# Attention in a hybrid decoder step: keys of the last branch unmasked, scores on quarter tiles, its projections in three pieces spread over later steps

## The chip, the core and the metric

One core of one Trainium2 chip runs the whole program. The metric is the device time of the program in microseconds, as the median of several runs. The trace is of one profiled execution. Engines: TensorE (PE, with its weight loads PEld), VectorE (DVE), ScalarE (ACT), GpSimd (POOL), and SyncE (SP), which issues most DMAs. Each engine runs its own list of instructions in order; semaphores tie the lists together.

## What is computed

Two layers over a prompt of 1024 tokens and 8 sample tokens, model width 1024, float32. Layer one is a gated delta rule with an MLP, and is not touched. Layer two is the attention treated here, and then an MLP of width 4096. The attention has three branches (window, dilation) = (128, 1), (512, 4), (2048, 16). Each has 8 query heads of width 64 in 2 groups that share one key and value head each:

```
q = (h @ w_q).reshape(N, L, N_BRANCH, KV_HEADS_B, GQA_B, HEAD_DIM_B)
s = einsum('nqhgd,nqkhd->nqhgk', q_blk, kg) * scale + bias      # keys at distance 0, d, .., window
p = exp(s - lse);  o = einsum('nqhgk,nqkhd->nqhgd', p, vg)
out = sum over branches of softmax(lse) * o;  mix = out @ w_o
```

`bias` is the slope of the head times the distance. With the dilation taken out by reordering the tokens by their residue, a query tile of 128 tokens reads one or two key tiles of 128 tokens.

## The kernel before

**Dense products.** A product of 128 output features is made for one of three pieces of the 1032 token columns (`CUTS`: 352, 352, 328). It has 8 k-steps (`KT`) of three matmuls each: high part of the weight by high and by low part of x, low part of the weight by high part of x. Weights stream from memory as units of 4 k-tiles x 512 columns in two halves into `w_raw`; `split_hi` (ScalarE, L603) and `split_lo` (VectorE, L1113) multiply by the gain and split them into a ring of 4 slots, `w_hi` and `w_lo`. `take` (VectorE, L1802) moves a finished product out of PSUM: keys to `k_mask`, values to `v_feat`, queries to `q_stage`, from where SP stores them to memory (`store_query`), and `load_query` brings a tile of 128 queries back as `q_tile`.

**Steps.** The attention runs in 26 steps. Step i treats query tile i in the order of `tile_of` (L99): 0 to 7 are branch 2 (one key tile each), 8 to 15 branch 1 (one key tile at even, two at odd), 16 to 23 branch 0 (16 has one key tile, the others two). The two halves `hs` of a tile are 4 heads each. For a tile: `scores` (TensorE, L2599) multiplies queries and keys, into PSUM banks 3 and 4; `biased` (VectorE, L1868) adds the bias and writes `prob`; `maxima` takes the row maxima; `exps` (ScalarE) the exponentials; `turn` (TensorE, L2614) transposes the probabilities into banks 5 and 6; `turned` copies them to `prob_t` (bank 5 ScalarE, bank 6 VectorE); `apply` (TensorE, L2622) multiplies with V into bank 7; `keep_outputs` (ScalarE, L989) copies to `out_t`, and `outputs_turn` transposes it back. From step 19 on `merge_turn` adds the merging of the three branches. TensorE's order within a step, written out by hand from L2679 on, is: turn half 0 of the tile before, scores half 1 of this tile, outputs_turn, fill, turn half 1, scores half 0 of the next tile, fill, apply, fill.

**Keys.** `k_mask` holds the keys twice, once per group, with zeros in the other group's 64 rows. One matmul of 128 rows by 128 queries then gives the scores of both groups side by side: 256 columns for one key tile and 512 for two. A call makes two of these (j). With one key tile both share a bank (3 for half 0, 4 for half 1); with two, each has its own, which VectorE frees singly.

**Fills.** There are three places per step, numbered 3 x step, + 1, + 2. `dense_done(place)` says how many k-steps of the remaining 30 products are done by then: 96 in places 0 to 17 (queries of branch 1), then 6 per place until 240 are done at place 41, in step 13. `GROUPS` orders them: queries of branch 1, queries of branch 0, keys and values of branch 0. They rotate over PSUM banks 0 to 2. From place 66 on (step 22) the fills are the output projection (`output_done`, L2575), whose weights, units 10 and 11 counted from `U_KVQ`, `SPLITS` splits at the end of steps 12 to 15. `LOADS` names the weight halves that SP loads at each step.

**The 8 samples.** Their single query is treated beside the steps: `samples_queries` (VectorE, step 14) signals `dense_done`, on which SP loads their keys, values and bias (1.8 MB) over x_hi; then come `samples_keys` and `samples_scores` (16), `samples_maxima` (16), `samples_shares` (17), `samples_turn` (18), `samples_apply` and `samples_outputs` (19). `decode_done` lets SP bring back x (`x_b`, 4.1 MB) in step 20. `store_keys(0)` follows in SP's list of step 14.

## Time and profile before

| | us |
|---|---|
| median of 3 runs (2721.39 to 2723.74) | 2722.85 |
| the profiled execution | 2721.97 |
| its span | 2720.2 |

Granted clock of TensorE over the span: 0.991 of 2.4 GHz. The attention's steps begin in the trace at these times (the first `turn` of a step, or for step 0 its first `scores`):

| step | 0 | 6 | 8 | 14 | 15 | 16 | 17 | 18 | 19 | 20 | 21 | 22 |
|---|---|---|---|---|---|---|---|---|---|---|---|---|
| us | 1632.17 | 1695.54 | 1721.41 | 1808.88 | 1818.63 | 1830.17 | 1849.10 | 1856.74 | 1870.20 | 1881.81 | 1894.05 | 1903.67 |

How to read the rows further down. A row of windows has the stretch, its length, then the busy time of PE, PEld, DVE, ACT and POOL with the number of instructions, the granted clock of PE as a share of 2.4 GHz, the busy share of the DMA engines and GB/s. In a timeline one fp32 matmul has two records, so `x4` is two matmuls; records of a pipelined engine overlap, so the time of a group is best read from the start of one to the start of the next. In the chain each row is start, duration and what ran or was waited for. SPq is the queue of DMA issues of SP.

### The profile page before, as it was taken

The page shows a single profiled execution, that of the slowest core. Times are in us where ns is not written, and L with a number is a line of the kernel's source. Part 1 is how long each engine was busy: PE and PEld are TensorE (multiplying, and loading weights), DVE is VectorE, ACT ScalarE, POOL GpSimd, SP SyncE. Part 2 cuts the span into 40 slices and gives each one's busy share as a digit, 9 for nine tenths or more (in the row PEclk, how much of TensorE's full clock was granted, in tenths as well). Part 3 has the DMA queues.
Part 4 walks back from the last instruction along what each step waited for, and adds up shares of the span by engine and source line. Part 5 has one row for each costly group of instructions (what it writes and reads, how often), then busy time and mean ns, then how long its engine had stood idle before and what let it go on. Part 6 is the DMA issues. An engine that isn't in the chain of part 4 may idle for free.

```text
span 2720.2 us, 48302 instructions
## 1 busy us (share of the span) xinstructions
PE 2638.9 (97%) x20476; PEld 2508.2 (92%) x20476; DVE 1553.1 (57%) x2961; ACT 827.6 (30%) x1870; POOL 66.6 (2%) x92
## 2 busy tenths in 40 slices
PE   7999999997899999999999999988999999999998
PEld 6999999996699999999999998864899999999997
DVE  6777777777575444444444736567764444444445
ACT  5444544543141211121112314345531112111211
POOL 0000000000300000000000000002200000000000
PEclk9999999998999999999999999998999999999999
DMA  3111101134311111111111234334111111111111
GB/s 142 48 42 41 41 20 32 34 119 164 106 47 63 47 47 39 56 47 47 40 55 47 97 101 118 96 116 134 59 47 47 47 47 47 47 47 47 47 32 63
DMA packets 81989, 174.32 MB, mean 64 GB/s; under 512 B 21681, under 2 KB 46801, under 8 KB 81060
## 3 DMA queue, kind: packets, MB, share of 16 engines
q1 hardware_dynamic: 73860, 162.72, 18.5%
q10 hardware_dynamic: 7920, 8.56, 1.0%
q8 instruction: 162, 2.65, 0.4%
q14 instruction: 47, 0.39, 0.0%
HBM read 140.28 MB, written 36.21 MB: 65 GB/s over the span
## 4 chain that ended last, share of the span: by engine, by line
PE 89%; DVE 5%; DMA 2%; ACT 1%; issue 1%; POOL 1%; SPq 0%; DVEq 0%; ACTq 0%; POOLq 0%
PE psum L2085 19%; PE psum L2086 19%; PE psum L2087 19%; PE psum L2159 4%; PE psum L2160 4%; PE psum L2161 4%; PE psum L2111 2%; PE psum L2358 2%; PE psum L2609 2%; PE psum L2567 1%; PE psum L2632 1%; PE psum L2568 1%; PE psum L2569 1%; PE psum L2450 1%; DMA x_half<-in_x 1%
## 5 line engine op out<-in xcount | busy, mean ns | idle before, releaser
L2085 PE MATMUL psum<-x_hi,w_hi 128*128 128x352 f32 (+1 forms) x1040 | 334.8, 322 | 0.0
L2086 PE MATMUL psum<-x_lo,w_hi 128*128 128x352 f32 (+1 forms) x1040 | 332.4, 320 | 0.0
L2087 PE MATMUL psum<-x_hi,w_lo 128*128 128x352 f32 (+1 forms) x1040 | 330.9, 318 | 0.0
L1118 DVE SCALAR_TENSOR_TENSOR w_lo<-w_raw,gains,w_hi 128x512 fp32r<-128x512 f32 x380 | 262.1, 746 | 84.7 <-ACT w_hi L608 84.6
L608 ACT ACTIVATE w_hi<-w_raw,gains 128x512 fp32r<-128x512 f32 x380 | 246.9, 712 | 121.5 <-DMA w_raw<-in_w 121.2
L2159 PE MATMUL psum<-x_hi,w_hi 128*128 128x352 f32 (+1 forms) x768 | 273.2, 356 | 1.2 <-DVE pre L1200 1.2
L2085 PE MATMUL psum<-u_hi_b,w_hi 128*128 128x352 f32 (+1 forms) x768 | 247.1, 322 | 0.0
L2085 PE MATMUL psum<-u_hi,w_hi 128*128 128x352 f32 (+1 forms) x768 | 246.7, 321 | 0.0
L2085 PE MATMUL psum<-x_hi_b,w_hi 128*128 128x352 f32 (+1 forms) x768 | 246.6, 321 | 0.0
L2160 PE MATMUL psum<-x_lo,w_hi 128*128 128x352 f32 (+1 forms) x768 | 245.9, 320 | 0.0
L2086 PE MATMUL psum<-x_lo_b,w_hi 128*128 128x352 f32 (+1 forms) x768 | 245.5, 320 | 0.0
L2161 PE MATMUL psum<-x_hi,w_lo 128*128 128x352 f32 (+1 forms) x768 | 245.2, 319 | 0.0
L2087 PE MATMUL psum<-u_hi_b,w_lo 128*128 128x352 f32 (+1 forms) x768 | 245.2, 319 | 0.0
L2087 PE MATMUL psum<-u_hi,w_lo 128*128 128x352 f32 (+1 forms) x768 | 245.2, 319 | 0.0
L2086 PE MATMUL psum<-u_lo_b,w_hi 128*128 128x352 f32 (+1 forms) x768 | 245.0, 319 | 0.0
L2086 PE MATMUL psum<-u_lo,w_hi 128*128 128x352 f32 (+1 forms) x768 | 245.0, 319 | 0.0
L2087 PE MATMUL psum<-x_hi_b,w_lo 128*128 128x352 f32 (+1 forms) x768 | 244.3, 318 | 0.0
L1742 DVE SCALAR_TENSOR_TENSOR relu<-psum,rs 128x352 f32<-128x352 f32 (+1 forms) x192 | 99.1, 516 | 214.2 <-PE psum L2087 206.7
L908 ACT ACTIVATE u_hi_b<-relu 128x352 fp32r<-128x352 f32 (+1 forms) x96 | 47.2, 492 | 519.4 <-DVE relu L1745 519.4
L908 ACT ACTIVATE u_hi<-relu 128x352 fp32r<-128x352 f32 (+1 forms) x96 | 47.2, 492 | 516.8 <-DVE relu L1745 516.8
L2086 PEld LDWEIGHTS psum<-x_lo,w_hi 128*128 128x128 f32 x1040 | 195.5, 188 | 0.5
L2085 PEld LDWEIGHTS psum<-x_hi,w_hi 128*128 128x128 f32 x1040 | 195.4, 188 | 0.5
(373 smaller groups left out, 5542.4 us busy)
## 6 DMA issues: line engine op xcount, KB each, us to landing
w_raw<-in_w SPq DMA_DIRECT2D x190, 512.0 KB, 3.7
q_tile<-scratch_q SPq DMA_DIRECT2D x24, 256.0 KB, 3.0
scratch_att<-o_out ACTq DMA_DIRECT2D x32, 132.0 KB, 2.5
x<-in_x SPq DMA_DIRECT2D x8, 516.0 KB, 9.8
s_state<-in_s_rec_in SPq DMA_DIRECT2D x2, 2048.0 KB, 14.7
out_s_rec<-s_state SPq DMA_DIRECT2D x8, 512.0 KB, 2.6
merge<-scratch_att SPq DMA_DIRECT2D x8, 512.0 KB, 3.7
scratch_o_heads<-head_out ACTq DMA_DIRECT2D x7, 512.0 KB, 2.7
```

The costliest lines, as they stand in the source:

```text
L608: done = act.activation(w_hi[:, slot, 2 * part + k], w_raw[:, part, k], ACT.Copy, scale=gains[:, unit * UW + 2 * part + k:unit * UW + 2 * ...
L908: act.activation(lay.u_hi[:, tile, THIRDS[third]], relu[:, 0:width(third)], ACT.Copy).then_inc(sem("u_hi_ready"), L.add("u_hi_ready"))
L1118: done = v.scalar_tensor_tensor(w_lo[:, slot, 2 * part + k], w_raw[:, part, k], gains[:, unit * UW + 2 * part + k:unit * UW + 2 * part + k ...
L1742: v.scalar_tensor_tensor(r, psum[:, TAKES[n % 6], 0:width(third)], 0.0, rs[:, cols], ALU.max, ALU.mult).then_inc(sem("product_free"), L.ad ...
L2085: mm(out, whi, xh[:, k, cols], start=k == 0, stop=False)
L2086: mm(out, whi, xl[:, k, cols], start=False, stop=False)
L2087: done = mm(out, wlo, xh[:, k, cols], start=False, stop=k == kts - 1)
L2111: done = nc.tensor.transpose(psum[0:cols, bank, at_col:at_col + rows], src, ident[0:rows, 0:rows])
L2159: mm(out, whi, x_hi[:, k, cols], start=k == 0, stop=False)
L2160: mm(out, whi, x_lo[:, k, cols], start=False, stop=False)
L2161: done = mm(out, wlo, x_hi[:, k, cols], start=False, stop=k == KT - 1)
L2358: done = mm(psum[out, bank + r, cols], lhs[rows, c, p], rhs(rows, c, p), start=True, stop=True, tile_position=(r * HD, c * HD))
```

## The change

The diff without the pieces that only rename or move addresses of the samples' buffers (these now lie as slices inside rows of x_hi and x_lo, their PSUM in bank 0 only; `merge` has room of its own, `k_feat` has half the size of `k_mask`). The samples' work moves one step ahead: keys, scores and maxima in 15, shares in 16, turn in 17, apply and outputs in 18; SP loads their own values in 16. `store_keys(0)` moves from SP's step 14 to 19. TensorE waits for `decode_done` at the first `merge_turn` (step 19) and not at the first output product.

```
 SPLITS = {1: ..., 10: ((9, 1, 1),),
-          12: ((10, 2, 0),), 13: ((10, 2, 1),), 14: ((11, 3, 0),), 15: ((11, 3, 1),)}
+          17: ((10, 2, 0),), 18: ((10, 2, 1),), 19: ((11, 3, 0),), 20: ((11, 3, 1),)}
 LOADS = {..., 8: ((9, 0),), 9: ((9, 1),),
-         10: ((10, 0),), 11: ((10, 1),), 13: ((11, 0),), 14: ((11, 1),), 15: ((12, 0),), 16: ((12, 1),),
+         10: ((10, 0),), 11: ((10, 1),), 18: ((11, 0),), 19: ((11, 1),), 20: ((12, 0),), 21: ((12, 1),),
          }
-GROUPS = ((4, (0, 1), 1), (4, (2, 3), 0), (2, (0, 1), 0))
+LATE = tuple((tiles, third, tile) for tiles, third in ((4, 2), (4, 0), (2, 2), (2, 0), (4, 1), (2, 1)) for tile in range(tiles))
+LATE_CUTS = (0, 384, 768, NT)

 def dense_done(place):
     if place < 18:
         return 8 + 88 * (place + 1) // 18 if place >= 0 else 0
-    return min(96 + 6 * (place - 17), 240)
+    if place < 41:
+        return 96 + 96 * (place - 17) // 23
+    return min(192 + 48 * (place - 40) // 13, 240)

 def dense_product(n):
+    if n < 12:
+        return 1, 4, (0, 1), n // 4, n % 4, CUTS
+    tiles, third, tile = LATE[n - 12]
+    return 0, tiles, (2, 3) if tiles == 4 else (0, 1), third, tile, LATE_CUTS
+
+def dense_bank(n):
+    return n % 3 if n < 12 else 1 + n % 2
...
         def load_query(i):
-            if tile == 0:
+            if tile == 0 or (b == 0 and tile == 3):
...
             def take(...):                                    # VectorE
                 if tiles == 2 and tile == 0:
-                    for g in range(2):
-                        rows = slice(g * HD, (g + 1) * HD)
-                        done = v.tensor_tensor(by_class(k_mask[rows, b % 2, g]), src[rows], scale[rows], ALU.mult)
-                        done.then_inc(sem(mark if g else "dve_order"), L.add(mark if g else "dve_order"))
+                    v.tensor_tensor(by_class(k_feat[:, b % 2]), src, scale, ALU.mult).then_inc(sem(mark), L.add(mark))
...
             def biased(nxt, hs):                              # VectorE
-                if nk == 1:
-                    v.wait_ge(sem(f"bank{3 + hs}_full"), L.next(f"bank{3 + hs}_full"))
-                    v.tensor_tensor(prob[:, par, hc(hs), P:2 * P], psum[:, 3 + hs].rearrange("p (n c) -> p n c", n=4),
-                                    bias[:, hc(hs), P:2 * P], ALU.add).then_inc(sem(f"bank{3 + hs}_free"), L.add(f"bank{3 + hs}_free"))
-                    return
-                for j in (2 * hs, 2 * hs + 1):
-                    ...                                       # one addition per bank, 128x512 each
+                cols = slice((2 - nk) * P, 2 * P)
+                def by_group(ap):
+                    return ap.rearrange("p (j g) c -> p g j c", g=2)
+                v.wait_ge(sem("scores_full"), L.next("scores_full"))
+                v.tensor_tensor(by_group(prob[:, par, hc(hs), cols]),
+                                psum[:, 3:5, 0:2 * nk * P].rearrange("p g (j c) -> p g j c", j=2),
+                                by_group(bias[:, hc(hs), cols]), ALU.add).then_inc(sem("scores_free"), L.add("scores_free"))
...
             def scores(nxt, hs):                              # TensorE
-                keys = k_mask[:, b % 2, :, (tile + 1 - nk) * P:(tile + 1) * P]
+                cols = slice((tile + 1 - nk) * P, (tile + 1) * P)
+                if nxt == tile_of(0) and hs == 0:
+                    for free in ("bank3_free", "bank4_free"):
+                        pe.wait_ge(sem(free), L.next(free)), L.skip(free, -1)
+                else:
+                    pe.wait_ge(sem("scores_free"), L.next("scores_free"))
                 for j in (2 * hs, 2 * hs + 1):
-                    bank = hs if nk == 1 else j % 2
-                    if nk == 2 or j % 2 == 0:
-                        pe.wait_ge(sem(f"bank{3 + bank}_free"), L.next(f"bank{3 + bank}_free"))
-                    lo = (j % 2) * 2 * P if nk == 1 else 0
-                    done = mm(psum[:, 3 + bank, lo:lo + 2 * nk * P].rearrange("p (g c) -> p g c", g=2), q_tile[:, par, j], keys,
-                              start=True, stop=True)
-                    if nk == 2 or j % 2:
-                        done.then_inc(sem(f"bank{3 + bank}_full"), L.add(f"bank{3 + bank}_full"))
+                    lo = j % 2 * nk * P
+                    for g in range(2):
+                        rows = slice(g * HD, (g + 1) * HD)
+                        for h in range(2):
+                            part = slice(h * HD, (h + 1) * HD)
+                            done = mm(psum[part, 3 + g, lo:lo + nk * P], q_tile[rows, par, j, part], k_feat[rows, b % 2, cols],
+                                      start=True, stop=True, tile_position=(g * HD, h * HD))
+                done.then_inc(sem("scores_full"), L.add("scores_full"))
...
             for step in range(STEPS):                         # TensorE
                 if cur:
                     turn(cur, 0, "q_tile_free" if step == 1 else None)
                 if step == 15:
                     pe.wait_ge(sem("kv_ready"), L.next("kv_ready"))
-                    transposes(5, values(0, 0))
-                if nxt:
-                    scores(nxt, 1)
+                    transposes(5, late_values(0, 3))
                 if step > 1:
                     outputs_turn(step)
                 if step:
                     fill(3 * step)
+                if nxt:
+                    scores(nxt, 1)
...
                 if cur:
                     turn(cur, 1, "q_tile_free")
+                if step == 18:
+                    pe.wait_ge(sem("kv_ready"), L.next("kv_ready"))
+                    transposes(5, late_values(3, 6))
                 if step < 23:
                     scores(tile_of(step + 1), 0)
                 fill(3 * step + 1)
```

In `LATE`, `(4, third)` are the four query products of branch 0 in one piece of columns, `(2, third)` its keys and values. So by place 41 the pieces 2 and 0 are there (tiles 0 to 2, 6 and 7, and the samples), and piece 1 (tiles 3 to 5) follows by place 53, in step 17.

## Rows read from the trace of the kernel before

**Rows 1.** The page, busy time and share of the span of each engine.
```profile
PE 2638.9 (97%) x20476; PEld 2508.2 (92%) x20476; DVE 1553.1 (57%) x2961; ACT 827.6 (30%) x1870; POOL 66.6 (2%) x92
```

**Rows 2.** Windows: steps 0-5, 6-13, 14-17, 18-21; busy us, clock, DMA share, GB/s.
```profile
1632.17:1695.54 63.37, 63.29 (x381) 56.13 (x381) 39.20 (x66) 30.41 (x118) 0.00 (x0) 1.00 0.45 123
1695.54:1808.88 113.34, 111.52 (x650) 93.79 (x648) 63.39 (x109) 41.37 (x144) 0.00 (x0) 1.00 0.27 82
1808.88:1856.74 47.86, 34.88 (x201) 19.96 (x198) 31.94 (x57) 23.53 (x82) 0.00 (x0) 0.89 0.44 135
1856.74:1903.67 46.93, 39.94 (x194) 23.22 (x193) 36.53 (x69) 25.87 (x86) 19.33 (x42) 0.93 0.53 167
```

**Rows 3.** Chain of waits, steps 14 to 21: start, duration, what it was.
```profile
1816.76 1.95 PE psum L2632 x8
1818.73 0.60 ACT v_feat L993
1819.33 1.23 ACT w_hi L608 x2
1820.59 1.41 DVE w_lo L1118 x2
...
1827.33 13.04 DMA q_tile<-scratch_q
...
1855.46 3.29 DMA merge_stats<-scratch_att
...
1891.12 3.00 PE psum L2632 x8
```

**Rows 4.** Waits of TensorE in steps 0 to 25: total us, times, longest.
```profile
PE psum L2609 <- DVE prob L1879: 7.6, 6, 2.9
PE psum L2111 <- DVE prob_t L1892: 4.9, 2, 4.7
PE psum L2632 <- DVE prob_t L1892: 4.8, 4, 2.3
...
PE psum L2609 <- DMA q_tile<-scratch_q: 2.0, 2, 1.3
```

**Rows 5.** Timeline of TensorE: start, duration, records, in steps 7, 8 and 22.
```profile
1717.40 1.08 PE L2632 MATMUL psum<-prob_t,v_keys 128*64 128x512 f32 x4
1718.41 0.43 PE L2567 MATMUL psum<-x_hi,w_hi 128*128 128x352 f32 x1
...
1721.84 1.03 PE L2609 MATMUL psum<-k_mask,q_tile 128*128 128x256 f32 x4
1722.71 0.60 PE L2111 MATMUL psum<-ident,v_feat 128*128 128x128 f32 x4
...
1904.60 1.88 PE L2609 MATMUL psum<-k_mask,q_tile 128*128 128x512 f32 x4
1906.32 0.60 PE L2111 MATMUL psum<-ident,v_feat 128*128 128x128 f32 x4
```

**Rows 6.** The same view in the first stage, around groups of quarter tiles (L2358).
```profile
88.84 0.69 PE L2358 MATMUL psum<-ident,pair 64*64 64x64 f32 x32
89.36 0.65 PE L2358 MATMUL psum<-pair 64*64 64x64 f32 x32
...
90.68 0.32 PE L2160 MATMUL psum<-x_lo,w_hi 128*128 128x352 f32 x1
90.84 0.32 PE L2161 MATMUL psum<-x_hi,w_lo 128*128 128x352 f32 x1
91.09 0.69 PE L2358 MATMUL psum<-dec,pair 64*64 64x64 f32 x32
...
91.98 0.32 PE L2160 MATMUL psum<-x_lo,w_hi 128*128 128x352 f32 x1
```

**Rows 7.** VectorE by shape, 1625 to 1950: count, busy us, mean ns.
```profile
L1873 DVE TENSOR_TENSOR prob<-psum,bias 128x512 f32<-128x512 f32 x26 | 17.8, 685 | 5.9 <-PE psum L2609 5.7
...
L1864 DVE TENSOR_TENSOR bias<-dist,slopes 128x1024 f32<-128x1024 f32 x5 | 5.9, 1222 | 0.2 <-DVE s_q L1834 0.2
```

**Rows 8.** Timeline of TensorE in the MLP: dense matmuls of 328 columns.
```profile
1300.48 0.32 PE L2086 MATMUL psum<-x_lo,w_hi 128*128 128x328 f32 x1
1300.63 0.32 PE L2087 MATMUL psum<-x_hi,w_lo 128*128 128x328 f32 x1
```

**Rows 9.** The page, DMA issues: count, KB each, median us to landing.
```profile
w_raw<-in_w SPq DMA_DIRECT2D x190, 512.0 KB, 3.7
...
merge<-scratch_att SPq DMA_DIRECT2D x8, 512.0 KB, 3.7
```

**Rows 10.** Timeline of SP's queue in step 14.
```profile
1812.91 0.35 SPq L526 DMA_DIRECT2D s_keys<-in_s_keys  x1
```

More of the change, by code:

```diff
@@ L1848, in attention_layer @@
                 if n == 0:
-                    for g in range(2):
-                        v.memset(k_mask[(1 - g) * HD:(2 - g) * HD, :, g], 0.0).then_inc(sem("dve_order"), L.add("dve_order"))
                     v.wait_ge(sem(L.last), L.value(L.last))
-                    v.sem_inc(sem("k_zeroed"), L.add("k_zeroed"))
+                    v.sem_inc(sem("k_begun"), L.add("k_begun"))
             kv_ready()
@@ L2539, in attention_layer, with late_values @@
                 stage_begin(n)
+            def late_values(first, last):
+                return [v_feat[:, 0, c * P:(c + 1) * P] for c in range(first, last)]
             def values(b, h):
@@ L2556, in fill @@
                     n, k = divmod(m, KT)
-                    g, tiles, slots, in_group = dense_product(n)
-                    third, tile = divmod(in_group, tiles)
-                    out, cols = psum[:, n % 3, 0:width(third)], THIRDS[third]
-                    if in_group == 0 and k == 0:
+                    _, _, slots, third, tile, cuts = dense_product(n)
+                    cols = slice(cuts[third], cuts[third + 1])
+                    out = psum[:, dense_bank(n), 0:cols.stop - cols.start]
+                    if n in (0, 12, 20) and k == 0:
                         pe.wait_ge(sem("raw_free"), L.next("raw_free", 4))
+                    if n == 12 and k == 0:
+                        L.skip("product_free")
                     if k == 0:
@@ L2723, in attention_layer @@
                 if m == 48:
-                    for free in ("bank5_free", "bank0_free", "bank3_free", "bank4_free"):
+                    for free in ("bank5_free", "bank0_free"):
                         pe.wait_ge(sem(free), L.next(free)), L.skip(free, -1)
+                    pe.wait_ge(sem("scores_free"), L.next("scores_free"))
                 output_step(m)
```

163 lines of the change are left out of this document (80 added, 83 removed).

## The prediction

> **What bounds the kernel now.** The page comes first: TensorE is busy for 97% of the span, so what shortens its stream shortens the kernel, except where it idles [rows 1]. The stages of the attention say where that is. I cut them at the starts of steps 0, 6, 14, 18 and 22. In steps 0 to 13 TensorE is busy for 174.8 of 176.7 us at a granted clock of 1.00. In steps 14 to 17 it is busy for 34.9 of 47.9 us and in steps 18 to 21 for 39.9 of 46.9, with the clock at 0.89 and 0.93 [rows 2]. So 20 us of the 23 us of idle time lie where no dense fills are left. Third, the chain of waits through these steps shows what they wait for: behind the product with V (L2632) stand ScalarE's copy (0.60), its half of a weight split (1.23), VectorE's half (1.41) and the bias addition, and only then the next scores; later a load of q_tile that takes 13.04 us and one of the merge statistics of 3.29 [rows 3]. The waits of TensorE in steps 0 to 25 have the same names: `prob` 7.6 us, `prob_t` 9.7, q_tile 2.0 [rows 4].
>
> I work with the profiled execution (2721.97 us, of which the span is 2720.2). The median of the runs is 0.9 us above it.
>
> **Scores on quarter tiles.** A call of `scores` had two fp32 matmuls of 256 columns (one key tile) or 512 (two); it now has 8 quarter matmuls of 128 or 256 columns. Old price: 1721.84 to 1722.71 is 0.87 us for one key tile, 1904.60 to 1906.32 is 1.72 for two [rows 5]; 1.72 us for 2 x 512 columns is 4 cycles of 2.4 GHz per column. The trace has quarter tiles in another stage: 16 fp32 quarters of 64 columns lie between the dense matmuls at 90.84 and 91.98, which is 1.14 us; less two dense slots of 0.16 they cost 0.82 [rows 6]. With all four quarters at work they would stream 16/4 x 64 columns x 4 cycles at 2.4 GHz = 0.43 us, so they do run together, and about 0.39 us per group is lost at entry and exit. A call of now streams 0.43 us for one key tile (8/4 x 128 columns x 4 cycles) and 0.85 for two. With 0.39 on top: 0.82 and 1.24. So a one-tile call gains 0.05 us and a two-tile call 0.48. Bounds: the loss per call can be nothing (then 0.44 and 0.87 gained) or, if 128x128 fp32 neighbours make it worse, 0.6 (then 0.16 lost and 0.27 gained). I take 0.39 because it is the same kind of group between the same neighbours.
>
> The Trainium skill, TensorEngine Tiling (Array Packing), Key Properties, says that a change of the tiling mode, not of the tile alone, drains TensorE; the 0.39 us of [rows 6] agree. By a count without that rule the forecast below would come out some 14 us lower.
>
> **A new wait, in every step.** Each call writes both banks 3 and 4 from column 0, and one semaphore, `scores_free`, hands them back after one VectorE addition. The first half of the next tile is issued right after the second half of this one, with only `turn(cur, 1)` between. TensorE waits there in its queue with the fill, `apply` and the next step behind it. Before, the old order had a fill and a turn between those two calls. Price: results land about 0.17 us after the stream (1.03 shown for a stream of 0.87) [rows 5]; 0.04 to VectorE; the addition 0.69 us for 512 elements, and for 1024 the 1.22 of `bias_of`, an addition of that size [rows 7]; 0.04 back; less the turn, 0.44 for one key tile and 0.87 for two. That is 0.50 us where both tiles have one key tile, 1.03 where the next has two and this one has one, and about 0 the other way. Some 0.15 us of the exit of the quarter mode lies under this wait, so 0.35 and 0.88. The old order's own wait for `prob` at the second half, which the fill now covers, goes. Lower bound 0 (if the latency is smaller than the turn), upper 0.6 and 1.2.
>
> **Stage by stage.**
> Steps 0 to 5, 63.4 us: step 0 has no turn or fill between its calls, which adds about 1.1 us; five waits of 0.35 add 1.8; 12 one-tile calls give back 0.6. +2.3.
> Steps 6 to 13, 113.3 us: the fills of 144 k-steps of three matmuls become 99. Three matmuls of 352 columns are 0.48 us at a pitch of 0.16, of 328 columns 0.45 at 0.15 [rows 6, 8], and the new pieces of 384, 384 and 264 have the same 1032 columns in all; mean 0.474. 45 x 0.474 = -21.3. Ten one-tile calls -0.5, six two-tile calls -2.9, idle time that goes -1.8 [rows 2], three waits of 0.35 and three of 0.88 +3.7. -22.8.
> Steps 14 to 17, 47.9 us, now full of TensorE work: the 45 k-steps and 12 entries of 0.1 make 22.5; turns 5.2, output turns 1.8; `apply` 2 x (1.12 + 1.97) = 6.2 (1.95 for two tiles in [rows 3], 1.01 for one in [rows 5], and an entry each); scores 3 x 0.82 + 5 x 1.24 = 8.7; two waits of 0.88; the samples' rows, scores and transposes and five transposes of late values 4.4. Sum 50.6. VectorE has 31.9 us of work in these four steps, 8 in each [rows 2], beside 12.5 of TensorE, and the splits that stood between its steps are gone from here. What is late next is the samples' load: SP stores query tile 24 before it looks at `dense_done`, and that product is taken only at the end of VectorE's step 14, so the four loads (1.8 MB, issued from 1812.91 on before [rows 10]) start about 3.5 us ahead of step 15, while VectorE wants them in step 15 and no longer in 16, in front of its second bias addition. Load time: nothing shows it alone; q_tile behind 1 MB of stores took 13 us [rows 3], a weight half (0.5 MB) takes 3.7 at the median [rows 9]. I take 9, which makes TensorE 2 us late; bounds 0 and 6. 52.6, or +4.7. The stall of 13.04 us behind the key store is gone, since the store moves to step 19.
> Steps 18 to 21, 46.9 us: no fill here, neither before nor after. The splits of the output weights move from steps 12 to 15 to steps 17 to 20. That of 17 is covered by the last fills and runs parallel to the merge load, which stalled this place before as well. Behind 18, 19 and 20 the chain `apply`, copy 0.60, split 1.23, split 1.41, addition 1.2 runs bare. Against the starts of the next additions in the old trace that is 3.7, 2.7 and 3.3 us = 9.7. Seven two-tile calls give back 3.4, of which I count half, since VectorE has the rest of the path. +8.0. Bounds: +3 if VectorE's own idle time takes most of it, +17 if each split costs its full 4.3 us and the clock falls to 1.2 GHz around it as it did in these steps (0.93 on the mean). The samples' `apply` (3.4 us) moves from 19 to 18, no change. The key store and two weight halves (2 MB) now share the queue with x_mid's 4.1 MB; before, `merge` (3.7 us at the median [rows 9]) and q_tile stood behind that without a wait longer than 1.3 us [rows 4], and the steps are longer now: 0, at worst +3.
> From step 22: three two-tile calls -1.4, one wait +0.4. -1.0.
> Less VectorE work (one full-width take of K for two half-width ones, no memset of the mask) lies beside TensorE: 0.
> Sum: +2.3 - 22.8 + 4.7 + 8.0 - 1.0 = -8.8; 2721.97 - 8.8 = 2713.2, as a median 2714. Own range 2709 to 2719.
>
> **Rivals.**
> 1. The quarters cost little more than their stream. For: a second group follows the first after 0.52 us [rows 6], 0.09 over the stream. Against: both groups there are in quarter mode; here each stands among full-width turns and fills. The 36 calls of steps 0 to 17 would give 0.3 us more each, 10.8: 2703.
> 2. The handover of banks 3 and 4 eats the gain: VectorE is not free when the scores land (its take of a product, 0.5 to 0.6 us, or the maxima stand first) and each step from 1 to 17 loses 0.5 us more, 8.5 in all: 2723, the same time. For: the additions keep their 0.69 and 1.22 us while the scores before them halve. Against: the takes stand ahead of the second addition and have the fill to finish in. The skill's page on tiling (PSUM Bottleneck) says that packing speeds up TensorE and not the emptying of PSUM, which is this rival's kind; no trace of before has it in these steps.
> 3. The splits behind 17 to 20, slower: TensorE idles longer in steps 18 to 20, its clock halves in them, and `apply` (3.00 at 1891.12 against 1.95 [rows 3]), turns and scores on the chain stretch too; each of four splits costs 4.3 + 1.9 us = 25 in place of 8: 2731. It decides once these steps grow by more than 17 us. For: clock and idle time of [rows 2]. Against: steps 14 to 17 had two such bare splits, and cost some 4 us each.
> 4. The load of the samples' keys holds VectorE in step 15, 6 us late in place of 2: 2718.
>
> **Chances.** Forecast 0.45 (rival 4 lies at its edge), rival 1 0.19, rival 2 0.20, rival 3 0.16. A measurement tells about 0.2% (5.4 us) from no change. Faster by more than that: 0.41 of the forecast and 0.19 = 0.60; within: 0.23; slower: 0.17. The range goes from 2702 to 2726: rival 1 with a little more, and rival 2 with part of rival 3.
>
> **What would show it.** Calls of `scores` at 0.8 and 1.2 us from start to the next group; a wait of scores on `prob` of 0.3 to 1.0 us in most steps; steps 6 to 13 at 91 us; steps 14 to 17 with TensorE over 90% busy at clock 1.00 and 52 us long; steps 18 to 21 at 55 us with `w_lo` in the chain between V's product and the next scores; no 13 us q_tile load in the chain. I am wrong if steps 6 to 13 shrink by less than 19 us, or steps 14 to 21 together grow by over 20.

## The result and the profile after

The changed kernel takes 2749.03 us (median of 4 runs, 2747.56 to 2751.28), the kernel before 2723.3 on the same chip: a ratio of 1.0093 (1.008 to 1.0105), slower by 25.7 us. I had forecast 2714 and a range up to 2726. The time lies outside that range, and the sign was wrong.

First the page of the changed kernel, busy time of each engine; it answers to [rows 1].

```profile
PE 2634.2 (96%) x21052; PEld 2505.7 (91%) x21052; DVE 1542.6 (56%) x2928; ACT 829.0 (30%) x1871; POOL 66.2 (2%) x92
```

TensorE is busy for 4.7 us less and the span is 25.6 us longer (2745.8), so what came is waiting. The windows of steps 0 to 5, 6 to 13, 14 to 17 and 18 to 21 (columns as in [rows 2]) say where.

```profile
1635.60:1702.21 66.61, 63.23 (x537) 53.41 (x537) 39.44 (x66) 30.40 (x118) 0.00 (x0) 0.97 0.42 119
1702.21:1795.13 92.92, 84.98 (x707) 66.60 (x705) 58.05 (x94) 39.15 (x140) 0.00 (x0) 0.98 0.29 86
1795.13:1866.36 71.23, 52.75 (x431) 41.80 (x430) 30.50 (x53) 21.72 (x81) 0.39 (x2) 0.86 0.28 80
1866.36:1927.74 61.38, 41.73 (x289) 27.19 (x287) 40.91 (x65) 30.97 (x93) 18.57 (x40) 0.81 0.54 171
```

Against [rows 2], with the forecast in brackets: steps 0 to 5 +3.2 us (+2.3), 6 to 13 -20.4 (-22.8), 14 to 17 +23.4 (+4.7), 18 to 21 +14.4 (+8.0), from 22 on +1.5 (-1.0), and 3.4 more ahead of step 0 (1635.60 against 1632.17). That last part can't be put down to the change: among the runs below, kernels that are the same up to step 0 reach it between 1631.9 and 1637.8 us. A stage with no edit in it mostly repeats to 0.5 us, so I compare stages; the exceptions are named. Over steps 0 to 21 the change costs 20.6 us, and it costs them from step 14 on.

In steps 14 to 17 one wait holds nearly all of it. TensorE's timeline in step 15 (start, duration, idle before and its releaser), and below it VectorE's:

```profile
1831.21 1.13 PE L2624 MATMUL psum<-k_feat,q_tile 64*64 64x128 f32 x16 [18.06 <-DVE prob L1886]
```

```profile
1829.62 0.32 DVE L1957 COPY s_high<-s_kv 128x8 f32<-128x8 f32 x3 [20.42 <-DMA s_low<-in_s_bias]
1829.85 1.22 DVE L1886 TENSOR_TENSOR prob<-psum,bias 128x1024 f32<-128x1024 f32 x1
```

TensorE waits 18.06 us for `prob`. But VectorE is not slow: it stands 20.42 us at L1957, the first of `samples_keys`, for the samples' constants, and `prob` is queued behind. Names in a wait are the last link only; the link before it is a DMA. SyncE's queue shows the four loads (start, duration of the issue):

```profile
1805.77 0.65 SPq L535 DMA_DIRECT2D s_high<-in_s_keys  x1
1806.46 0.67 SPq L535 DMA_DIRECT2D s_high<-in_s_va  x1
1807.17 1.36 SPq L535 DMA_DIRECT2D s_high<-in_s_vb  x1
1808.58 17.23 SPq L535 DMA_DIRECT2D s_low<-in_s_bias  x1
```

and two windows (the last two columns are DMA share and GB/s) what the queues moved:

```profile
1808.00:1812.00 4.00, 4.00 (x40) 3.52 (x38) 0.69 (x1) 2.45 (x9) 0.00 (x0) 1.00 1.04 307
1815.00:1825.00 10.00, 0.00 (x0) 0.00 (x0) 0.00 (x0) 0.00 (x0) 0.00 (x0) 0.55 0.07 21
```

First 307 GB/s at a full share, then 21 GB/s at a share of 0.07, about one sixteenth. So I read that one of the core's 16 DMA engines works alone for 10 us and more, and the issue of the last load stands 17 us behind it. No compute engine is busy in that window.

When the wait is over TensorE runs at half clock for a while. Its granted clock, the number ahead of the DMA share, is 0.50 over the next 4.8 us, which costs about 2.4 us more:

```profile
1831.20:1836.00 4.80, 4.79 (x28) 4.44 (x28) 2.95 (x5) 2.08 (x8) 0.00 (x0) 0.50 0.43 133
```

Steps 18 to 21 by single steps (same columns):

```profile
1866.36:1886.66 20.30, 16.45 (x96) 12.11 (x95) 10.45 (x19) 7.70 (x24) 4.98 (x12) 0.66 0.28 80
1886.66:1900.43 13.77, 8.42 (x66) 5.02 (x64) 9.85 (x15) 7.76 (x23) 4.59 (x11) 0.88 0.41 127
1900.43:1914.08 13.65, 8.43 (x66) 5.03 (x64) 9.76 (x15) 7.76 (x23) 4.49 (x10) 0.87 0.55 157
1914.08:1927.74 13.66, 8.44 (x67) 5.03 (x65) 10.86 (x16) 7.76 (x23) 4.51 (x10) 0.88 1.04 365
```

Before they were 13.46, 11.61, 12.24 and 9.62 us. The chain of waits through step 19 into step 20 shows a closed loop:

```profile
1895.80 1.28 POOL part L1117
...
1897.17 0.69 DVE merged L1936
1897.86 0.61 DVE prob_t L1899
1898.47 0.09 issue
1898.57 1.95 PE psum L2646 x8
...
1901.09 1.33 ACT w_hi L618 x2
...
1902.45 1.41 DVE w_lo L1133 x2
1903.86 1.15 DVE prob L1886
```

V's product, ScalarE's copy of the outputs (`k_feat` 0.60 in all), `w_hi`, `w_lo`, and only then the next tile's `prob`.

### The profile page after: what moved, and what is told of

Read it like the earlier page. It is cut to its first block, busy times and chain, and to the rows that moved or that the text cites. A ratio compares the mean times of both kernels' runs of the same rounds, so it can differ in the third digit from the quotient of the medians.

```text
span 2745.8 us, 49374 instructions
## 1 busy us (share of the span) xinstructions
PE 2634.2 (96%) x21052; PEld 2505.7 (91%) x21052; DVE 1542.6 (56%) x2928; ACT 829.0 (30%) x1871; POOL 66.2 (2%) x92
## 4 chain that ended last, share of the span: by engine, by line
PE 87%; DVE 6%; DMA 3%; issue 1%; ACT 1%; POOL 1%; SPq 0%; DVEq 0%; ACTq 0%; POOLq 0%
PE psum L2091 19%; PE psum L2092 19%; PE psum L2093 19%; PE psum L2165 4%; PE psum L2166 4%; PE psum L2167 4%; PE psum L2364 2%; PE psum L2117 2%; PE psum L2578 1%; PE psum L2646 1%; PE psum L2624 1%; PE psum L2456 1%; PE psum L2579 1%; PE psum L2580 1%; DMA x_half<-in_x 1%
```

## The experiments

Stage lengths in us, cut at the same instructions in every trace. They are those of one profiled execution, whose own time stands in the column "traced"; "time" is the median of all runs of that kernel. The two can lie some us apart (e7 by 6.0, e14 by 4.4, e15 by 4.7), and the ratio goes by the medians.

| kernel | 0-5 | 6-13 | 14-17 | 18-21 | from 22 | traced | time | ratio to before |
|---|---|---|---|---|---|---|---|---|
| before | 63.4 | 113.3 | 47.9 | 46.9 | 816.5 | 2722.0 | 2723.3 | |
| after | 66.6 | 92.9 | 71.2 | 61.4 | 818.1 | 2747.6 | 2749.0 | 1.0093 (1.008 to 1.0105) |
| e1_pad | 66.7 | 92.7 | 57.7 | 61.5 | 818.1 | 2733.6 | 2736.8 | 1.0052 (1.0035 to 1.0069) |
| e2_early | 66.7 | 93.0 | 65.1 | 60.9 | 818.1 | 2738.8 | 2739.1 | 1.0065 (1.0048 to 1.0082) |
| e3_order | 61.7 | 90.9 | 66.8 | 63.1 | 818.1 | 2737.2 | 2737.2 | 1.0051 (1.0036 to 1.0067) |
| e4_split | 66.7 | 93.0 | 71.6 | 61.6 | 818.4 | 2746.6 | 2744.6 | 1.0073 (1.0056 to 1.009) |
| e6_padorderearly | 61.7 | 91.2 | 50.0 | 63.6 | 818.0 | 2718.6 | 2721.5 | 0.999 (0.998 to 1.0) |
| e7_smallsplits | 68.0 | 92.0 | 57.3 | 56.6 | 818.9 | 2732.4 | 2726.3 | 1.0009 (0.9997 to 1.002) |
| e8_quarters | 66.6 | 110.9 | 46.1 | 47.9 | 818.1 | 2726.8 | 2727.9 | 1.0012 (1.0003 to 1.0021) |
| e9_quartersorder | 61.7 | 107.1 | 45.8 | 47.9 | 818.1 | 2715.5 | 2719.1 | 0.9983 (0.9975 to 0.9992) |
| e10_hifirst | 66.5 | 92.7 | 71.1 | 55.9 | 817.6 | 2743.7 | 2743.2 | 1.0059 (1.0046 to 1.0072) |
| e11_all | 61.7 | 91.0 | 50.0 | 56.7 | 818.1 | 2713.3 | 2714.1 | 0.9957 (0.9943 to 0.9971) |
| e12_lolater | 61.7 | 91.0 | 50.0 | 48.3 | 818.8 | 2706.0 | 2705.5 | 0.9933 (0.9919 to 0.9947) |
| e13_sapply | 61.7 | 91.1 | 59.2 | 44.3 | 818.1 | 2708.7 | 2709.7 | 0.9951 (0.9937 to 0.9965) |
| e14_84rows | 68.0 | 93.5 | 58.2 | 66.4 | 817.6 | 2741.5 | 2737.1 | 1.0046 (1.003 to 1.0062) |
| e15_before84 | 63.4 | 113.3 | 45.6 | 45.6 | 817.1 | 2720.3 | 2725.0 | 0.9999 (0.999 to 1.0008) |

**e1_pad: the load in 128 rows.** `s_vb` goes to 83 partitions in pieces of 512 bytes (it lies in s_high now, with other data between); before it went to 83 whole rows of 4 KB. Here it is padded to 128 rows.

```
-  ... (s_vb, "s_vb"), (s_bias, "s_bias")):
+  ... (s_high[:, :, P:2 * P], "s_vb"), (s_bias, "s_bias")):
   sp.dma_start(dst[:], t[name]
```

> The values of the samples' old keys (the load into s_vb) are padded from 83 to 128 rows, in memory and in the load; the extra rows are zeros that nothing reads. Theory: the 18 us wait of the scores in step 15 comes from this one load, which after its issue runs at 20 to 22 GB/s, one sixteenth of the DMA engines' busy time, because 83 rows of 8 pieces are not dealt over the engines; with 128 rows it runs at over 200 GB/s, all four loads land within 8 us of the first issue, the wait falls from 18 to about 3 us and the time by some 15 us, to 2734. Rival: the small pieces of all four loads and the queue in front of them are the cause; then the load takes as long as now or longer (more bytes), and the time stays at 2749.

Steps 14 to 17 fell from 71.2 to 57.7 us, VectorE's wait from 20.42 to 6.70 and TensorE's from 18.06 to 4.34. Counted from step 0, VectorE is released 13.8 us sooner though more bytes are loaded; whether 83 rows or their 512-byte pieces had been the trouble stayed open.

**e14_84rows and e15_before84: one row more.** The changed kernel and the kernel before, each with `s_vb` in 84 rows (one of zeros) in place of 83; in e14 the pieces stay 512 bytes, in e15 whole rows of 4 KB. The lines below are those of e15; e14 loads into `s_high[0:SB + 1, :, P:2 * P]`.

```
-    s_vb = at("s_vb", [SB, NS, P], F32, a)
+    s_vb_rows = at("s_vb", [SB + 1, NS, P], F32, a)
+    s_vb = s_vb_rows[0:SB]
```

> The changed kernel with s_vb padded by one row of zeros only, 84 rows in place of 83, its pieces of 512 bytes as they are. Theory a, the count of rows decides how many DMA engines share the load: steps 14 to 17 fall from 71.2 to 58 or 59 us (57.7 with 128 rows), TensorE's wait of 18.06 in step 15 to about 5, the whole to 2737. Theory b, the short pieces or the part of a row decide: steps 14 to 17 stay at 71, the whole at 2749. The Trainium skill, DMA: Bandwidth & Descriptors, on why a DMA increments its semaphore by 16, states that a load runs on the largest number of engines up to 16 that divides its outermost dimension: 1 for 83, 14 for 84; that is theory a.

> The kernel before with s_vb in 84 rows of 4 KB in place of 83, nothing else. Theory a: its load was on one engine too, only hidden, since VectorE wanted it 22 us later; the window behind it that moves 44 GB/s at a share of 0.14 goes, and of the loads behind it q_tile no longer takes 13.04 us. What that gives is bounded by the waits of steps 14 to 17 (one of 4.67 us for prob_t, one of 1.26 for q_tile): steps 14 to 17 fall from 47.9 to 43 to 47, the whole by 1 to 5 us. Theory b: whole rows were dealt over all engines before, nothing changes, q_tile still takes 13 us.

One row of zeros did what 45 had done: steps 14 to 17 take 58.2 us, and TensorE's wait is 4.6. So it is the count of rows, not their pieces. And it was so before as well, though the time hardly shows it. From the DMA issues of 1810 to 1842 (count, KB, median us to landing), first before, then e15:

```profile
out_p_v<-v_feat SPq DMA_DIRECT2D x1, 512.0 KB, 13.6
out_s_kv_new<-s_kv SPq DMA_DIRECT2D x1, 24.0 KB, 21.4
```
```profile
out_p_v<-v_feat SPq DMA_DIRECT2D x1, 512.0 KB, 6.2
out_s_kv_new<-s_kv SPq DMA_DIRECT2D x1, 24.0 KB, 8.3
```

24 KB that take 21.4 us to land were a sign that stood in the trace of before, and so was this window of it, 44 GB/s at a share of 0.14 with much still to land:

```profile
1821.00:1823.00 2.00, 0.35 (x1) 0.30 (x2) 2.00 (x4) 0.04 (x1) 0.00 (x0) 1.00 0.14 44
```

q_tile's 13.04 us of [rows 3], which I had read as the key store's, left the chain as well (2.9 us is the median of the three q_tile loads there). The time of e15 is that of before: 0.9999 (0.999 to 1.0008), with 2.2 us less in steps 14 to 17. There the slow load was nearly hidden, because VectorE wanted it some 24 us after its issue (1813.77 to 1837.90); the change left it no cover.

The Trainium skill (DMA: Bandwidth & Descriptors, on why a DMA increments its semaphore by 16) states this rule: a load runs on the largest number of engines up to 16 that divides the size of its outermost dimension, in its source and in its destination. For 83, a prime, that is 1, for 84 it is 14 and for 128 it is 16. The shares and the two pairs of runs agree; I had not applied it.

**e2_early: the same load, sooner.** SyncE issues the four loads ahead of the store of the last query tile before them.

```
+ if step == 14:
+     sp.wait_ge(sem("dense_done"), L.next("dense_done"))
+     for dst, name in (...): sp.dma_start(dst[:], t[name]) ...
  for place in range(3 * step, 3 * step + 3):
      ... store_query(...)
```

> SP issues the samples' four loads at the head of its step 14, before it stores query tile 24, instead of behind it. Theory of a slow load: the issue comes 7 us earlier (1798.5 in place of 1805.8), the load takes its 21 us as before, the wait in step 15 falls from 18 to about 11 us: 2742. Rival: the load is slow because it meets the query store and the q_tile load in the queue; then it lands in 8 us when it starts ahead of them, and the wait goes nearly: 2733.

Steps 14 to 17 came to 65.1. The load starts at 1795.26 here; the stores and q_tile loads stand behind its issue (17.78 us for `s_bias`), and TensorE now waits 12.19 us for q_tile in place of `prob`. An earlier start gives 6 us; the rest moves to whoever is next in the queue.

```profile
1796.66 1.26 SPq L526 DMA_DIRECT2D s_high<-in_s_vb  x1
1797.97 17.78 SPq L526 DMA_DIRECT2D s_low<-in_s_bias  x1
1815.80 0.42 SPq L475 DMA_DIRECT2D scratch_q<-q_stage  x1
1819.99 0.37 SPq L484 DMA_DIRECT2D q_tile<-scratch_q  x1
```

**e3_order: the next tile's first scores behind the second fill.**

```
-                if step < 23:
-                    scores(tile_of(step + 1), 0)
                 fill(3 * step + 1)
+                if step < 23:
+                    scores(tile_of(step + 1), 0)
```

> TensorE issues the first half of the next tile's scores behind the second fill of a step, and not in front of it, so that the fill stands between the two calls that share banks 3 and 4. Theory: the waits of scores on the bias addition (0.32 us in each step with one key tile, 0.4 to 0.9 in others, some 6 us in steps 1 to 17 beside the 18 us one) go under the fill: 2744. Rival: they only move, since the first addition of the next step comes later by the length of the fill and the second call then waits for it: 2749 or slower. The stretch from step 0 to 6 tells it best: 66.6 us now, 65 by the theory.

Steps 0 to 5 fell from 66.6 to 61.7 us, under the 63.4 of before, and steps 6 to 13 from 92.9 to 90.9. Steps 14 to 17 gained 4.4, 2.6 of them in the wait for the load; steps 18 to 21 lost 1.7. So most of what the handover of banks 3 and 4 cost goes once a fill stands between the two calls.

**e4_split: splits and loads one step sooner** (16 to 19 in place of 17 to 20, loads of units 11 and 12 from step 17).

```
-          17: ((10, 2, 0),), 18: ((10, 2, 1),), 19: ((11, 3, 0),), 20: ((11, 3, 1),)}
+          16: ((10, 2, 0),), 17: ((10, 2, 1),), 18: ((11, 3, 0),), 19: ((11, 3, 1),)}
```

> The splits of the output weights come one step earlier (16 to 19 in place of 17 to 20) and their loads too (17, 18; 19, 20 for the MLP's first unit). Theory: every split behind a step without fills puts copy, two split halves and addition between one product with V and the next scores, so one bare split fewer (18 and 19 in place of 18, 19 and 20) takes 3.5 to 4 us from steps 18 to 21 (61.4 us now): 2745. Rival: those steps are bound by VectorE and GpSimd's merging anyway, and the time stays at 2749.

Steps 18 to 21 stayed at 61.6: the step with no split any more (21) fell to 11.1, but 19 and 20 rose from 13.8 and 13.7 to 15.5 and 15.4, since V's product took 3.63 and 3.68 us there in place of 1.95. It isn't shown that the edit did that: e14, whose code from step 16 on is that of the changed kernel, shows 15.4, 15.4 and 15.3 for steps 19 to 21 in its trace, with the product at 3.58 us.

**e6_padorderearly: the first three repairs together**, the edits of e1, e2 and e3.

> The changed kernel with the three repairs together: the samples' values of sequence b padded to 128 rows in memory and in their load, SyncE issuing the samples' four loads ahead of the store of the last query tile before them, and the first half of the next tile's scores behind the dense work of the step instead of ahead of it. If the losses are separate, the stages add up from the single runs: steps 0 to 5 61.7, 6 to 13 90.9, 14 to 17 57.7 less the 4.3 of wait that padding left, some 52, 18 to 21 63.1, from 22 on 818.1; with the attention's start at 1634 that is a span of 2720 and a time near 2721.5, within 3 us of the kernel before. If they share one slack (the rival), steps 14 to 17 stay at 57 and the time at 2727.

2721.5 us; stages 61.7, 91.2, 50.0, 63.6. They do add up: with padding, the earlier issue and the new order, no wait of TensorE over 1 us is left in steps 14 to 17. The ratio, 0.999 (0.998 to 1.0), is no change that can be told.

**e7_smallsplits: the bare splits an eighth as long.** With padding; ScalarE and VectorE split 64 of 512 columns of units 10 and 11, and the rest of these weights is left out of the result.

```
+            cols = slice(0, 64 if unit in (U_KVQ + 10, U_KVQ + 11) else HALF)
...
-    done = act.activation(w_hi[:, slot, 2 * part + k], w_raw[:, part, k], ACT.Copy,
+    done = act.activation(w_hi[:, slot, 2 * part + k, cols], w_raw[:, part, k, cols], ACT.Copy,
```

> The changed kernel with padding, and with the splits of units 10 and 11 of the output weights (steps 17 to 20) cut to 64 of their 512 columns in ScalarE and VectorE: the rest of these weights is left unsplit, a part of the computation that is left out; the instructions, waits and loads stay. If bare splits cost what lies in the chain (1.23 w_hi and 1.41 w_lo of steps 18 to 20), steps 18 to 21 fall from 61.5 to about 53. If the stage is long because of TensorE's granted clock and the samples' apply (6.8 us in step 18 at clock 0.66), it stays within 2 us of 61.5, with the waits of 3.1 us shorter and TensorE's own spans longer.

The trace fits neither. Step 18 fell from 20.3 to 15.4 us, while steps 19, 20 and 21 are 13.8, 13.7 and 13.7, as with full splits. Its chain of waits:

```profile
1894.14 3.70 PE psum L2648 x8
1897.87 0.04 issue
1897.91 0.60 ACT k_feat L1007
1898.51 0.48 ACT w_hi L619 x2
1899.02 0.48 DVE w_lo L1135 x2
1899.50 1.15 DVE prob L1888
```

Two things are seen. The splits shrank from 2.74 to 0.96 us in the chain, and V's product is at the long one of its two lengths, 3.70 (granted clock 0.75 in step 21, 0.88 in the changed kernel's), which takes it all back in this execution. And `prob` still starts 1.6 us after the product has ended, behind two instructions that do almost nothing. In e9_quartersorder, with no split there, `prob` for that half was done under the product (1883.95, beside 1883.26 to 1886.54), and step 21 takes 9.05. So the split's place in the queues costs too. That is the new theory.

It doesn't show that length costs nothing, for the traced execution is the second slowest of e7's ten: 2732.4 us at a granted clock of 0.983 over the span, while the median is 2726.3 and the three fastest are 2721.0 to 2723.6 at 0.989 to 0.990. e1_pad, which differs from e7 by the full-length splits alone, has a median of 2736.8. By the medians the shorter splits save 10.5 us, more than the 8.5 that the theory of their length had given. The ratios to before (1.0009 against 1.0052) say the same, and so do the ranges (2721.0 to 2734.9 against 2733.6 to 2741.0).

**e8_quarters and e9_quartersorder: the scores alone.** The kernel before, with quarter tiles, the joint handover and the second half's scores behind the first fill; in e9 also the order of e3.

```
+                    for g in range(2):
+                        for h in range(2):
+                            done = mm(psum[part, 3 + g, ...], q_tile[rows, par, j, part], k_feat[rows, b % 2, cols], ...,
+                                      tile_position=(g * HD, h * HD))
+                done.then_inc(sem("scores_full"), ...)
```

> The kernel before, with the scores on quarter tiles alone (keys without zeroed halves, one handover of both banks per half, the second half's scores behind the step's first dense fill): pieces, splits, loads and samples are those of before. My theory: a half's call of 0.60 or 1.02 us plus waits of 0.3 to 0.9 us for the handover costs as much as the streams that it saves; steps 0 to 5 go from 63.4 to 66.6 as in the changed kernel, steps 6 to 13 by +1 to +3, the whole by +4 to +9, 2727 to 2732. The rival: quarter tiles are free or a gain, and the 3.2 us of steps 0 to 5 came from the transfers and the larger pieces: the whole within 2 us of 2723.

> The kernel before with the scores on quarter tiles, and the first half of the next tile's scores behind the step's second dense fill. If the order alone made the loss of steps 0 to 5 (66.6 to 61.7 in the run of the order on the changed kernel), they come to 61.7 here, 1.7 below before, steps 6 to 13 to 2 us below 113.3, and the whole to 2718 to 2721: the best so far. If bare steps (18 on) lose what dense ones gain, because a handover has nothing beside it there, steps 18 to 21 grow by 2 to 4 and the whole stays at 2723.

e8 gives steps 0 to 5 the 66.6 us of the changed kernel: the whole loss of that stage comes from the quarters with their handover and order, not from the larger pieces or their transfers. The other stages change by -2.4, -1.7, +1.0 and +1.5, and the time by 3.3 us or 0.12%, less than my theory had. With the order of e3 the stages are 61.7, 107.1, 45.8, 47.9, and the time 2719.1, a ratio of 0.9983 (0.9975 to 0.9992). My forecast for that run held in the time and in steps 0 to 5; in steps 6 to 13 the gain was 6.2 us where I had 2. The 1.5 us from step 22 on belongs to the quarters too; why wasn't tried.

**e10_hifirst and e11_all: `w_hi` ahead of the wait for V's product.** e10 is the changed kernel with this alone, e11 has all four repairs.

```
-                if cur:
+                if cur and step < 17:
                     keep_outputs(step)
 ...
                 for unit, slot, half in SPLITS.get(step, ()):
                     split_hi(U_KVQ + unit, slot, (half,))
+                if cur and step >= 17:
+                    keep_outputs(step)
```

> The changed kernel, with one reordering on ScalarE from step 17 on: the high part of a weight half (w_hi) is computed ahead of keep_outputs, which waits for the step's apply, instead of behind it. Nothing else is moved. New theory: what a bare split costs is its place and not its length (cut to an eighth it left steps 19 to 21 at 13.7 us each): ScalarE reaches it only behind the copy of the apply's outputs, VectorE waits 4.1 us for it with the next tile's biased scores queued behind, and so the step's chain cannot start before the apply has ended. With w_hi ahead of that wait, steps 19, 20 and 21 fall from 13.8, 13.7 and 13.7 to near 12.0, 12.0 and 9.1 (the steps without a split in the kernel before with quarter tiles), step 18 from 20.3 to 15 to 17; steps 18 to 21 from 61.4 to 48 to 51, the whole to 2736 to 2739. The rival, length or the clock: VectorE's own 1.41 and TensorE at half clock keep the steps at 13 and over, steps 18 to 21 stay above 56.

> The changed kernel with all four repairs: padding, early load, the first half's scores behind the second dense fill, and w_hi ahead of keep_outputs from step 17 on. By the first theory of the run before it, 2721.5 less the 10 to 15 us that steps 18 to 21 lose: 2707 to 2712, under the kernel before and under the kernel before with quarter tiles (2719). By the rival, 2716 to 2721.

Steps 18 to 21 fell from 61.4 to 55.9 (19.9, 13.6, 12.0, 10.4), half of what I had expected, at the rival's edge; e11_all came to 2714.1, between the 2707 to 2712 of the theory and the 2716 to 2721 of the rival. e10's chain shows what is left: `w_hi` is early, but VectorE still takes `w_lo` ahead of `prob`.

```profile
1898.95 1.33 ACT w_hi L618 x2
1900.30 1.41 DVE w_lo L1135 x2
1901.71 1.15 DVE prob L1888
```

**e12_lolater: `w_lo` behind the next half's `prob` and maxima.** e11 and:

```
                 if nxt:
                     biased(nxt, 0)
                     maxima(step, nxt, 0)
+                if 18 <= step:
+                    for unit, slot, half in SPLITS.get(step - 1, ()):
+                        split_lo(U_KVQ + unit, slot, (half,))
```

> The kernel with the four repairs, and VectorE's low part of a split (w_lo, 1.42 us in a row) moved from the end of steps 17 to 20 to behind the first half's biased scores and maxima of the next step. In the chain of waits of the four repairs w_hi 1.23 and w_lo 1.42 still stand ahead of prob in each of these steps. If place is what costs, w_lo now lies beside TensorE's calls: steps 18 to 21 fall from 56.7 to 50 to 52, the whole from 2714 to 2708 to 2710. If it only delays the prob_t copy behind it instead (the rival), they stay at 55 to 57 and the whole at 2713 to 2715.

Steps 18 to 21 are 48.3 us (15.6, 9.1, 12.6, 11.0) and the time is 2705.5 us, 0.9933 of before (0.9919 to 0.9947): better than both kernels, and than I had expected (50 to 52, and 2708 to 2710). The same full-length splits, in another place, cost 15.3 us less than in e6 (63.6). Step 19 alone, by its window:

```profile
1852.47:1861.53 9.06, 6.96 (x67) 4.28 (x65) 7.21 (x13) 7.36 (x23) 4.30 (x9) 1.00 0.64 193
```

**e13_sapply: the samples' product in step 17.** e12, with `samples_apply()` moved from step 18 to ahead of step 17's product with V, to find whether its 6.8 us are the clock's.

```
-                if step == 18:
-                    samples_apply()
...
+                if step == 17:
+                    samples_apply()
                 if cur:
                     apply(cur)
```

> The run before it, with the samples' apply moved from step 18 (no dense work; 6.8 us at a granted clock of 0.66 in the changed kernel) to step 17, ahead of that step's apply, while dense work still runs. If its length is the granted clock's, it takes 3.4 us there, as in the kernel before, and steps 14 to 21 together shrink by about 3.4 us, the whole to 2705. If the wait for the samples' turned shares shows instead, step 17 grows by as much as step 18 shrinks, and nothing is gained.

2709.7, 4.3 us slower than e12: step 17 grew by 9.2 and steps 18 to 21 shrank by 4.0. TensorE's timeline tells why (each of the first rows is one matmul of 8 columns, then come V's product and the last fill):

```profile
1832.87 0.36 PE L2696 MATMUL psum<-s_low,s_high 128*128 128x8 f32 x2 [1.19 <-ACT s_low L1040]
1833.09 0.37 PE L2697 MATMUL psum<-s_low,s_high 83*128 83x8 f32 x2
...
1834.73 0.57 PE L2697 MATMUL psum<-s_low,s_high 83*128 83x8 f32 x2
1835.16 0.57 PE L2696 MATMUL psum<-s_low,s_high 128*128 128x8 f32 x2
...
1838.65 1.98 PE L2652 MATMUL psum<-prob_t,v_keys 128*64 128x512 f32 x4
1840.56 0.69 PE L2584 MATMUL psum<-x_hi,w_hi 128*128 128x384 f32 x1
1841.05 0.52 PE L2585 MATMUL psum<-x_lo,w_hi 128*128 128x384 f32 x1
```

It begins at a pitch of 0.22 us a row and goes on at 0.43. Ahead of it stood dense work, a call of `scores` and an idle 1.19 us; the clock falls during the run of tiny matmuls, and the fill behind them then goes at a pitch of 0.32 in place of 0.17. In e12 the same product takes 3.6 us in step 18 (1841.13 to 1844.73, pitch 0.22), and the clock falls only behind it: V's product of that step takes 3.68. So the length is the clock's, but my remedy was wrong: here the halved clock fell on V's product and the fill, and nothing was gained. What brings the clock down in the one place and not in the other is open.

## Why the prediction was wrong

**The samples' load.** The term was "Load time: nothing shows it alone ... I take 9, which makes TensorE 2 us late; bounds 0 and 6." It decided the case: from the first issue at 1805.77 to VectorE's release at 1829.60 the load takes 23.8 us, and TensorE is 18.06 late. The start was near ("about 3.5 us ahead of step 15"; it was 2.1, from 1805.77 to 1807.88), and right was "VectorE wants them in step 15 and no longer in 16"; what failed is that I priced 1.8 MB by bytes, from rows of other transfers, and took 13 us for a stall behind stores when it was this load's own shadow. Rival 4 named the place and the wait, with 6 us a third of the size.

**Steps 14 to 17 otherwise.** "Sum 50.6" of TensorE's work holds: 71.2 us less the wait of 18.06 and the 2.4 of half clock behind it leave 50.8. In e1, too, 4.8 us at a granted clock of 0.50 (1816.60 to 1821.40) follow a wait of only 4.34. So the load cost 20.5 us where the sum has 2, and that the clock would fall behind a wait was in no term of it. With the load out of the way and the calls in e3's order, e6, e11 and e12 show 50.0. Full cover was right.

**Steps 18 to 21.** "Behind 18, 19 and 20 the chain `apply`, copy 0.60, split 1.23, split 1.41, addition 1.2 runs bare" is the chain shown above, link by link. "+8.0", as 9.7 less 1.7, came out as 14.4. Steps 19 to 21 grew by 2.2, 1.4 and 4.0, though the samples' product of 3.4 us left step 19: 11.0 for the three splits less what the two-tile calls give, against 8.0. The other 3.4 is the samples' product in step 18, from 1873.82 to 1880.66, 6.8 us at a granted clock of 0.66 over the step, which I had as "(3.4 us) moves from 19 to 18, no change"; in e12 it takes 3.6. The size was off by 3 us on each, and the reason for the first was incomplete: what a bare split costs hangs on its place. Where the changed kernel has it, its length counts in full (e7 against e1_pad, 10.5 us by the medians); in e12 the same full splits leave this stage at 48.3, where e9, with no split in it, has 47.9. The high part must not stand behind the copy of V's product, nor the low part ahead of the next `prob`. Rival 3 ("its clock halves in them") named what takes back 1.7 us a step in e4, e7 and e14; in the changed kernel's own trace it did so in step 18 alone.

**Steps 6 to 13.** "45 x 0.474 = -21.3" with the rest gave -22.8; measured -20.4, so the mechanism and the size of the main gain held and my bound of 19 wasn't crossed. The missing 2.4 us are not the handover's: its waits sum to 2.3 us here, in steps 6, 9, 11 and 13 (0.32, 0.66, 0.50, 0.85), where I had set 3.7. But TensorE waits 5.2 us more for other things that the sum has at nothing: 1.08 for q_tile, 2.0 in three waits for `prob_t` and the exponentials, and 2.12 in step 8, where VectorE computes the new `bias` (2.36 us) ahead of the addition that frees the banks. That last one stays when the call is moved (2.1 in e3). The calls give back a little more than I had set (below).

**Steps 0 to 5 and the new wait.** +2.3 forecast, +3.2 measured. By e8 it is the whole effect of the quarters and their handover. Step 0 makes 2.2 of it (10.07 against 7.84; I had 1.1): two waits of 0.88 and 0.91, and the first matmuls behind them at a lower clock. In steps 1 to 5 the wait is 0.32 us (forecast 0.35), as the timeline shows:

```profile
1650.18 0.67 PE L2624 MATMUL psum<-k_feat,q_tile 64*64 64x128 f32 x16 [0.32 <-DVE prob L1886]
```

The price of a call was nearly right. In e3, where nothing waits, a one-tile call stands between a dense matmul and a turn:

```profile
1656.17 0.32 PE L2580 MATMUL psum<-x_hi,w_lo 128*128 128x352 f32 x1
1656.41 0.67 PE L2624 MATMUL psum<-k_feat,q_tile 64*64 64x128 f32 x16
1657.01 0.66 PE L2117 MATMUL psum<-ident,prob 128*128 128x128 f32 x4
1657.42 0.41 PE L2578 MATMUL psum<-x_hi,w_hi 128*128 128x352 f32 x1
1657.67 0.33 PE L2579 MATMUL psum<-x_lo,w_hi 128*128 128x352 f32 x1
```

From start to start the call takes 0.60 us, 0.17 over its stream of 0.43. But the 0.39 of [rows 6] had been read from a dense matmul ahead of the group to the second one behind it, and so holds the entry and the exit too. Read in that way the stretch is 1.50 us (1656.17 to 1657.67), and the same stretch with a turn alone takes 0.76 (1645.51 to 1646.27 in the changed kernel). The call costs 0.74 us, against 0.82 forecast and 0.87 before, and it loses 0.31, not 0.39. A two-tile call takes 1.02 from start to start and 1.17 in this way (1736.85 to 1738.78 in e9, less 0.76), against 1.24 and 1.72. So a one-tile call gains 0.13 us and a two-tile call 0.55, where I had 0.05 and 0.48. Rival 1, "The quarters cost little more than their stream", isn't borne out. The Trainium skill (TensorEngine Tiling (Array Packing), Key Properties) states that a change of tiling mode drains TensorE; the 0.31 us lost at each call agree. The calls' gain lay under the handover's wait until e3 moved the call; only then do both show, and the quarters turn from 0.12% slower (0.03 to 0.21) into 0.17% faster (0.08 to 0.25).

**From step 22.** -1.0 forecast, +1.5 measured, in e8 too (23 is 13.7 in place of 11.7, 22 is 12.0 in place of 13.0). Not explained.

Of my own marks for being wrong the second came true: steps 14 to 21 together grew by 37.8 us, where I had set 20. The expected gain was there, and three things gave it back, the load in 83 rows, the two calls with nothing between them and the place of the splits: e12, which keeps every part of the change and moves these, has a ratio of 0.9933, e9, which has the quarter tiles and their order alone, 0.9983.

## What to carry to other kernels

When a change takes the cover off a transfer, price it from its rows and from how long things behind it take to land, not by its bytes; a DMA share near one sixteenth, or 24 KB that need 21 us, is a sign that one engine carries that transfer or one ahead of it. When an in-order engine gets work that nothing covers, ask what stands behind it and what that was hidden under: ahead of the long wait and behind the critical instruction its cost can go to nothing. And a wait that comes from two calls in a row is often removed by moving one of them past work that is there anyway.

## What the runs showed of the hardware

- A load of 83 rows (332 KB) ran at 21 GB/s and a share of 0.07 of the 16 DMA engines, as on one of them; with 84 rows VectorE's wait behind it fell from 20.42 to 6.94 us, with 128 to 6.70.
- A call of 8 quarter matmuls between full-width neighbours took 0.60 us at 128 columns and 1.02 at 256 from start to start, and 0.74 and 1.17 with the delays at its entry and exit. VectorE's addition over both banks (128x1024) still took 1.22 us.
- TensorE's granted clock has two levels, full and half (2.4 and 1.2 GHz), and V's product took 1.95 or 3.6 to 3.7 us by them. In steps 19 to 21 the same code showed the one in the changed kernel's trace (13.8, 13.7, 13.7 us a step) and the other in e14's (15.4, 15.4, 15.3): 5 us of the time that no edit explains (e14's traced execution, 2741.5 us, is the slowest of its four; the others took 2736.5 to 2737.4). Step 0 differs likewise (10.1 us, 11.5 in e7 and e14).
- After a wait of 18.06 us, and of 4.34 in e1, TensorE ran the next 4.8 us at a granted clock of 0.50.
- In e13 the clock fell in the middle of a run of 16 matmuls of 8 columns (pitch 0.22 to 0.43 us), 1.19 us of idle time behind dense work and a call of `scores`.
